# Gated decoder step: natural panels cut as half the contraction by 512 columns, with four token tiles open at once

## The chip, the cores and the metric

The kernel runs on one core of a Trainium2 chip. The metric is the device time of one execution in microseconds (us), here the median of three runs.

## The reference, cut to what matters

One layer for 512 prompt tokens and 8x4 sample tokens, all in float32:

```
h = rmsnorm(x, g_mix);  z = h @ w_in          # 1024 x 7680: [u | va | q | k | v | gate_a | gate_b]
a = gelu(u) * (tril(W_s) @ rmsnorm(gelu(va)) + b)
q, k = rotary(rmsnorm(q, g_q)), rotary(rmsnorm(k, g_k))          # 3 groups x 8 heads x 64
b = softmax over windows of the three groups (dilation 1, 4, 16; samples against cached keys and values)
x += (sigmoid(gate_a) * (a @ w_oa) + sigmoid(gate_b) * (b @ w_ob)) @ w_o
x += relu(rmsnorm(x) @ w_ff1)**2 @ w_ff2
x += sigmoid(rmsnorm(x) @ w_ple_gate) * (p @ w_ple_proj)
```

The new keys and values of the prompt, and the caches of the samples moved on by four positions, are outputs too.

## The kernel before

TensorE (PE) multiplies in split precision: each float32 operand is a rounded part (`_hi`) and a rest (`_lo`), and a product is hi·hi + lo·hi + hi·lo, so three matmuls. ScalarE (ACT) casts a weight half-panel of 128x2x512 or 128x1024 numbers from `w_raw` to `w_hi`, VectorE (DVE) subtracts to get `w_lo`; both buffers hold one panel in two halves of `w_hi`/`w_lo`.

The **natural stage** (us 14 to 346 of the profile) computes q, k and v of three groups and then va, with tokens on the partitions of the result. Its 20 panels are 1024 contraction rows by 256 columns; a pair of panels is one kind of one group (q0, k0, v0, q1, k1, v1, q2, k2, v2, va). A panel has three units: two of two 128-token tiles (48 matmuls of 128x256, lines 1321 to 1323) and one of the sample tokens (16 matmuls with 64 weight columns, lines 1329 and 1330). A unit's output is the PSUM bank `gm[:, u % 3]`: the bank that unit u fills is one that unit u-3 left, and PE waits for `unit_out` at the start of each unit. Scores of the attention (`kT`, `qT`) go to `psS` and to the fourth bank `gm[:, 3]`, transposes to `psT`, value products to `psO`. The profile names `psS` and `psO` alike: `psSO`.

Each engine walks slots written out by hand. In slot s ACT moves unit s out of PSUM (`z<-gm`), squares the heads with a read of the accumulator behind each (`sq<-z`), casts the next half-panels if the slot has them, copies transposes (`PT`, `qT`, `kT`), value products (`O`), and for each score piece exponentiates it (`prob`, twice 128x256 in group 0, four times 128x128 in groups 1 and 2) and writes the mask for the next piece into the bank. DVE multiplies by gain and rotates (`fin`, lines 1820 to 1833), takes row maxima of scores (line 1895), scales by the norm (line 1841), splits `w_lo` (line 1708) and works off one or two **chunks** of the samples' cached keys or values (1024 wide, two instructions each); a table of digits says how many chunks a slot has. `fin` has two buffers; those of k are stored to `kvp` by DMA, and a new rotation waits for the store of two tiles ago (`fin_stored0`, `fin_stored1`). The small PE steps of slot s (transposes `qk` and `pt`, scores, value products) are issued between the matmuls of unit s+1. The stage has 60 slots; the next stage (u, gates, output products) follows, with its own slots and the rest of the chunks, up to us 513. Then comes the feed-forward part, which the change leaves as it is.

```
for job in TJOBS.get(s, []): take_transposes(job)      # ACT, in slot s: behind evacuation, squares and casts
for job in SJOBS.get(s, []): ...                       # then exponentials and masks of the pieces of slot s
```

Of the kernel before, what the change touches and what calls it, by code (L numbers as in the profile page):

```python
# [24 lines left out]
D, SEQ, NB, T = 1024, 512, 8, 4  # L25
# [23 lines left out]
COLS = {"oa": 512, "ob": 512, "pj": 1024}  # L49
UNITS = []  # L50
for _p, (_kind, _g, _i) in enumerate(PANELS):
    _n = 3 if _kind in NATURAL else COLS.get(_kind, 256) // 128
    UNITS += [(_p, _kind, _g, _i, _s) for _s in range(_n)]
U_FF = len(UNITS)
NFF = 4
# [4 lines left out]
for _u, (_p, _kind, _g, _i, _s) in enumerate(UNITS):  # L60
    UNIT[_kind, _i * (COLS.get(_kind, 256) // 128) + _s if _kind not in NATURAL else (_g, _i, _s)] = _u
# [3 lines left out]
def summed_by_act(u):  # L65

    return UNITS[u][1] in ("k", "q")

# [29 lines left out]
def panel_end(p):  # L98

    if p < P_FF:  # L100
        return max(u for u in range(U_FF) if UNITS[u][0] == p) + 1
    return U_FF + 2 * (p - P_FF + 1)

# [76 lines left out]
def late_split(s):  # L180

    _, kind, _, _, sub = UNITS[s]
    return sub == 0 and (kind in NATURAL or kind == "oa")


def stores_heads(u):

    _, kind, g, _, sub = UNITS[u]
    return sub == 2 or (kind == "k" and not (g == 0 and sub == 0))
# [4 lines left out]
PIECE_SLOT = [18 + j for j in range(16)] + [36 + j for j in range(8)] + [54 + j for j in range(8)]  # L194
S_AT = {s: j for j, s in enumerate(PIECE_SLOT)}


def paired(j):

    return j < 30  # L200


def score_bank(j):

    return j % 2 if paired(j) else 0


NEXT_IN_BANK = {j: next((x for x in range(j + 1, len(PIECES)) if score_bank(x) == score_bank(j)), None) for j in range(len(PIECES))}
MASKED_BY_ACT = [x for x in NEXT_IN_BANK.values() if x is not None]

# [3 lines left out]
for _g in range(NG):  # L214
    for _kind in ("keys", "values"):
# [3 lines left out]
CHUNKS_IN_SLOT = ("000000000101202202102102102102213122102102102102112111"  # L219
                  "112103121010030112010100120313200000000000")  # L220
# [20 lines left out]
COPY_AT = [s for s in range(0, 96, 3) if s not in (48, 51, 54, 57)] + [97, 99, 100, 102]  # L241
V_BACK = {35: (1, 0), 39: (1, 1), 53: (2, 0), 57: (2, 1)}


X_STEPS = {10: (2,), 13: (3,), 14: (4,)}
# [4 lines left out]
def _plan_tjobs():  # L250
    n = 0
    order = []
    for s in range(SLOTS):
        if s >= 2 and UNITS[s - 2][1] in ("k", "q") and UNITS[s - 2][4] < 2:
            order.append((s, ("qk", s - 2)))
        if s - 1 in S_AT:
            order.append((s, ("pt", S_AT[s - 1])))
        if s == 53:
            order.append((s, ("ws",)))
        if s == 65:  # L260
            order += [(s, ("mixs",))] + [(s, ("mix", g)) for g in range(4)]
        if s == KEYS_END[2] + 1:
# [7 lines left out]
        if s == 77:  # L270
            order += [(s, ("bt", c)) for c in range(2)]
        if s == 78:
            order += [(s, ("bt", c)) for c in range(2, 4)]
        if 88 <= s < 96:
            order.append((s, ("x", s - 88)))
        if s == 95:
            order.append((s, ("xs",)))
        if 96 <= s < 98:
            order.append((s, ("p", s - 96)))
        if s == 98:  # L280
# [14 lines left out]
def _plan_sjobs():  # L295
    n = 0
    for s in range(SLOTS):
        jobs = []
        if s in S_AT and not (paired(S_AT[s]) and S_AT[s] % 2):
            jobs.append(("piece", S_AT[s]))  # L300
            if paired(S_AT[s]):
                jobs.append(("piece", S_AT[s] + 1))
        for job in jobs:
# [8 lines left out]
def small_steps(s):  # L312

    t, sc = TJOBS.get(s, []), [x for x in SJOBS.get(s, []) if not (paired(x[1]) and x[1] % 2)]
    steps = [("transposes", x) for x in t if x[0] == "qk"] + [("scores", x) for x in sc if x[0] == "piece"]
    steps += [("transposes", x) for x in t if x[0] != "qk"] + [("scores", x) for x in sc if x[0] != "piece"]
# [2223 lines left out]
```

## Time and profile before

| | before |
|---|---|
| median of 3 runs | 1040.69 us (1040.42 to 1045.89) |
| profiled execution, span | 1041.0 us |
| PE busy | 1023.5 us |
| DVE busy | 774.4 us |
| ACT busy | 518.5 us |
| natural stage, 14.14 to 346.00 | 331.86 us, of it PE 328.35, DVE 285.55, ACT 223.25 |
| 346 to 513 | 167.00 us, of it PE 162.82, DVE 150.22 |

The profile comes from one execution, 0.3 us above the median of the runs. Matmuls are pipelined, so a matmul's own duration is longer than the distance to the next; the distance from start to start is what one costs.

### The profile page before, as it was taken

The page shows a single profiled execution, that of the slowest core. Times are in us where ns is not written, and L with a number is a line of the kernel's source. Part 1 is how long each engine was busy: PE and PEld are TensorE (multiplying, and loading weights), DVE is VectorE, ACT ScalarE, POOL GpSimd, SP SyncE. Part 2 cuts the span into 40 slices and gives each one's busy share as a digit, 9 for nine tenths or more (in the row PEclk, how much of TensorE's full clock was granted, in tenths as well). Part 3 has the DMA queues.
Part 4 walks back from the last instruction along what each step waited for, and adds up shares of the span by engine and source line. Part 5 has one row for each costly group of instructions (what it writes and reads, how often), then busy time and mean ns, then how long its engine had stood idle before and what let it go on. Part 6 is the DMA issues. An engine that isn't in the chain of part 4 may idle for free.

```text
span 1041.0 us, 20872 instructions
## 1 busy us (share of the span) xinstructions
PE 1023.5 (98%) x8310; PEld 1008.5 (97%) x8310; DVE 774.4 (74%) x1004; ACT 518.5 (50%) x1253; POOL 245.6 (24%) x381
## 2 busy tenths in 40 slices
PE   9999999999999999999999999999999999999997
PEld 7999999999999999999999989999999999999997
DVE  6679888988899878999674368747856875786553
ACT  6773797658845574352264385414522531453332
POOL 2441233122312003958201211100100100012300
PEclk9999999999999999999999999999999999999999
DMA  6557556776687765776843335655664574573412
GB/s 186 192 178 231 200 177 208 227 242 206 208 256 213 210 218 148 224 218 186 258 142 122 122 122 208 214 183 172 229 209 152 195 247 168 171 252 130 162 54 86
DMA packets 131634, 195.89 MB, mean 188 GB/s; under 512 B 32321, under 2 KB 109473, under 8 KB 129746
## 3 DMA queue, kind: packets, MB, share of 16 engines
q1 hardware_dynamic: 107616, 125.51, 37.9%
q0 software_dynamic: 10560, 63.28, 18.3%
q10 hardware_dynamic: 13362, 5.77, 2.0%
q8 instruction: 66, 1.08, 0.4%
q14 instruction: 30, 0.25, 0.1%
HBM read 185.55 MB, written 62.00 MB: 238 GB/s over the span
## 4 chain that ended last, share of the span: by engine, by line
PE 66%; DVE 13%; ACT 5%; issue 5%; DMA 5%; POOL 3%; SPq 3%; ACTq 0%; DVEq 0%; POOLq 0%
PE gm L1347 26%; PE gm L1603 7%; PE psSO L1603 4%; PE gm L1321 4%; PE gm L1322 3%; PE gm L1323 3%; PE psT L1603 3%; DMA w_raw<-in_w_in 3%; PE psSO L1651 2%; PE psSO L1347 2%; PE psT L1347 2%; PE psT L1651 2%; DVE w_lo L1708 2%; POOL kv L2363 2%; ACT prob L1123 2%
## 5 line engine op out<-in xcount | busy, mean ns | idle before, releaser
L1321 PE MATMUL gm<-w_hi,h_hi 128*128 128x256 f32 x640 | 186.9, 292 | 1.1 <-DVE w_lo L1708 0.9
L1322 PE MATMUL gm<-w_hi,h_lo 128*128 128x256 f32 x640 | 180.8, 282 | 0.0
L1323 PE MATMUL gm<-w_lo,h_hi 128*128 128x256 f32 x640 | 180.1, 281 | 0.0
L1347 PE MATMUL gm<-h_hi,w_hi 128*128 128x272 f32 x624 | 132.7, 294 | 0.4 <-ACT z L852 0.4
L1347 PE MATMUL gm<-h_hi,w_lo 128*128 128x272 f32 x624 | 130.0, 290 | 0.0
L1347 PE MATMUL gm<-h_lo,w_hi 128*128 128x272 f32 x624 | 129.4, 289 | 0.0
L1321 PEld LDWEIGHTS gm<-w_hi,h_hi 128*128 128x128 f32 x640 | 120.8, 189 | 3.1 <-issue 1.7
L1323 PEld LDWEIGHTS gm<-w_lo,h_hi 128*128 128x128 f32 x640 | 121.2, 189 | 0.0
L1322 PEld LDWEIGHTS gm<-w_hi,h_lo 128*128 128x128 f32 x640 | 120.6, 188 | 0.0
L2352 POOL DMA_DIRECT2D out_kvs<-in_cache_kv_w x64 | 35.0, 547 | 345.2 <-PE gm L1347 120.6
L1708 DVE TENSOR_TENSOR w_lo<-w_raw,w_hi 128x1024 fp32r<-128x1024 f32 x76 | 90.5, 1228 | 21.3 <-ACT w_hi L755 20.8
L1347 PEld LDWEIGHTS gm<-h_hi,w_hi 128*128 128x128 f32 x624 | 98.1, 190 | 1.5 <-ACT z L852 0.6
L1347 PEld LDWEIGHTS gm<-h_lo,w_hi 128*128 128x128 f32 x624 | 98.6, 190 | 0.0
L1347 PEld LDWEIGHTS gm<-h_hi,w_lo 128*128 128x128 f32 x624 | 98.2, 190 | 0.0
L755 ACT CAST w_hi<-w_raw 128x1024 fp32r<-128x1024 f32 x76 | 76.8, 1046 | 30.4 <-DMA w_raw<-in_w_in 16.5
L765 ACT CAST w_hi<-w_raw 128x1024 fp32r<-128x1024 f32 x49 | 50.2, 1048 | 82.6 <-PE psSO L1347 28.5
L1347 PE MATMUL gm<-x_hi,w_hi 128*128 128x272 f32 x384 | 80.4, 291 | 0.0
L1347 PE MATMUL gm<-x_hi,w_lo 128*128 128x272 f32 x384 | 79.6, 289 | 0.0
L1347 PE MATMUL gm<-x_lo,w_hi 128*128 128x272 f32 x384 | 79.3, 288 | 0.0
L2363 POOL DMA_DIRECT2D kv<-in_cache_kv_w x128 | 69.4, 708 | 32.8 <-DVE acc L1954 16.8
L1721 DVE TENSOR_TENSOR w_lo<-w_raw,w_hi 128x1024 fp32r<-128x1024 f32 x49 | 59.0, 1221 | 11.9 <-ACT w_hi L765 11.8
L1347 PEld LDWEIGHTS gm<-x_lo,w_hi 128*128 128x128 f32 x384 | 60.4, 189 | 0.0
(378 smaller groups left out, 2662.7 us busy)
## 6 DMA issues: line engine op xcount, KB each, us to landing
out_kvs<-in_cache_kv_w POOLq DMA_DIRECT2D x64, 510.0 KB, 4.7
w_raw<-in_w_in SPq DMA_DIRECT2D x60, 512.0 KB, 6.2
w_raw<-in_w_ff SPq DMA_DIRECT2D x36, 512.0 KB, 5.7
kv<-in_cache_kv_w SPq DMA_DIRECT2D x128, 128.0 KB
kv<-in_cache_kv_w SPq DMA_DIRECT2D x64, 256.0 KB
out_kvs<-in_cache_kv_w POOLq DMA_DIRECT2D x32, 508.0 KB, 5.3
w_more<-in_w_ff SPq DMA_DIRECT2D x26, 512.0 KB, 6.1
kv<-in_cache_kv_w POOLq DMA_DIRECT2D x128, 64.0 KB, 3.3
```

Of the source, the lines that this page charges most:

```text
L755: nc.scalar.copy(w_hi[:, r, hh * 1024:(hh + 1) * 1024], w_raw[:, hh]).then_inc(w_hi_done, 1)
L765: nc.scalar.copy(w_pair(w_hi, PAIRS[p] + n).rearrange("p (k n) -> p k n", k=4), raw(p, hh)).then_inc(w_hi_done, 1)
L1321: nc.tensor.matmul(out, lh, wh, start=k == 0, stop=False)
L1322: nc.tensor.matmul(out, ll, wh, start=False, stop=False)
L1323: last = nc.tensor.matmul(out, lh, wl, start=False, stop=k == KD - 1)
L1347: last = nc.tensor.matmul(pair[:, half, 0:HALF], w, x[:, k0 + k, half * HALF:(half + 1) * HALF], start=first, stop=end)
L1603: last = nc.tensor.matmul(bank[:, 0:HALF], w[wx][:, k], x[xx][:, k], start=start and k == 0 and wx == xx, stop=k == 3 and wx == 1, skip_gr ...
L1651: last = nc.tensor.matmul(banks(u + sub)[:, half, 0:HALF], w, x[:, k, half * HALF:(half + 1) * HALF], start=first, stop=end, skip_group_ch ...
L1708: vec.tensor_tensor(w_lo[:, r, cols], w_raw[:, hh], w_hi[:, r, cols].bitcast(F32), ALU.subtract).then_inc(w_lo_done, 1)
L1721: vec.tensor_tensor(w_pair(w_lo, x).rearrange("p (k n) -> p k n", k=4), raw(p, hh), w_pair(w_hi, x).rearrange("p (k n) -> p k n", k=4).bit ...
L2352: pool.dma_start(dst, src).then_inc(cache_copied, 16)
L2363: pool.dma_start(dst, src).then_inc(late_landed[n % RING], 16)
```

## The change

A natural panel is now 512 contraction rows by 512 columns, so a pair of panels is the two halves of the contraction for all columns of one kind and group. A pair has five **sections** on PE: x=0 is tiles 0 and 1 over the first half, x=1 tiles 2 and 3 over the first half, x=2 the samples over both halves, x=3 tiles 0 and 1 over the second half, x=4 tiles 2 and 3 over the second half. Each tile has its own bank `gm[:, tile]`, open from x=0 or x=1 to x=3 or x=4. Samples go to `psO`, scores to `psS` and `psO`, value products to `psT`. There are 50 natural slots instead of 60. ACT and DVE handle in slot s the unit of two slots ago, in the order samples, t0, t1, t2, t3: tile 2 comes out in slot x=0 of the following pair and tile 3 in its slot x=1. The half-panel for the first half of the next pair is split in slot x=3, the other in slot x=0. Squares of tile 0 and of the samples are one wide Square, summed by DVE; those of tiles 1 to 3 stay as they were. The chunk table has 54 chunks in the natural slots instead of 60, the other six come later. The diff's core:

```diff
+SAMPLES = 4
+TILES = (SAMPLES, 0, 1, 2, 3)
+    elif _i == 1:
+        UNITS += [(_p, _kind, _g, 0, _a) for _a in TILES]
+        SLOT += [(_p - (_x < 2), _kind, _g, 0, _x) for _x in range(5)]
+OUT_OF = {_s: [_s - 2] if 2 <= _s < N0 else [N0 - 2, N0 - 1, N0] if _s == N0 else [_s] if _s > N0 else [] for _s in range(U_FF)}
...
-    return sub == 0 and (kind in NATURAL or kind == "oa")
+    return sub in (0, 3) if s < N0 else sub == 0 and kind == "oa"
...
-PIECE_SLOT = [18 + j for j in range(16)] + [36 + j for j in range(8)] + [54 + j for j in range(8)]
+PAIR_SLOT = [14, 18, 19, 23, 24, 28, 29, 33, 34, 38, 39, 43, 44, 48, 50, 52]
+PT_SLOT = [16, 19, 21, 24, 26, 29, 31, 34, 36, 39, 41, 44, 46, 49, 51, 53]
+PV_SLOT = [17, 20, 22, 25, 27, 30, 32, 35, 37, 40, 42, 45, 48, 50, 52, 54]
...
-CHUNKS_IN_SLOT = ("000000000101202202102102102102213122102102102102112111"
-                  "112103121010030112010100120313200000000000")
+CHUNKS_IN_SLOT = ("00000" "00012" "11213" "22111" "02101" "11213" "22111" "02101" "11213" "21101"
+                  "1211" "1013" "0112" "0102" "1113" "03132000" "00000000")
...
+            def natural_tiles(s):
+                    a = 2 * (x % 3) + n
+                    out, tile = gm[:, a], slice(128 * a, 128 * a + 128)
+                    if half == 0 and first:
+                        pe.wait_ge(unit_out, first - 5 + TILES.index(a) + 1)
...
+                        if n == 0 and x == 0:
+                            panel_split(p, 512, kk)
```

In all, 1,920 matmuls of 128x256 become 960 of 128x512, and 320 sample matmuls of 256 columns become 160 of 512; ACT has 1050 instructions before and 938 after, DVE 1006 and 976.

**ACT, slots 24 and 25** (end of pair k1, start of v1; `PT` is the copy of transposed probabilities, `prob` an exponential, `psSO<-masks` a mask, `z<-gm` the evacuation of tile 2). After the change:

```order
L983 COPY PT<-psT 128x512 [waits t_ready] x2
L1153 ACTIVATE prob<-psSO,O_blk 128x256 [waits t_ready,max_ready]
L1153 ACTIVATE prob<-psSO,O_blk 128x256
L1047 CAST psSO<-masks 128x512 [waits const_in,exp_done]
L1153 ACTIVATE prob<-psSO,O_blk 128x256 [waits t_ready,max_ready]
L1153 ACTIVATE prob<-psSO,O_blk 128x256
L870 COPY z<-gm 128x512 [waits z_used,ssq_ready,unit_ready,exp_done]
L848 ACTIVATE sq,st<-z 128x64 [waits fin_ready,unit_out]
L848 ACTIVATE sq,st<-z 128x64 x7
L782 CAST w_hi<-w_raw 128x1024 [waits unit_ready,w_landed00]
L782 CAST w_hi<-w_raw 128x1024 [waits w_landed01]
L970 COPY kT_59<-psT 128x16x32 [waits t_ready]
```

A place of before with two pieces ahead of an evacuation:

```order
L1123 ACTIVATE prob<-psSO,O_blk 128x256 [waits t_ready,max_ready]
L1123 ACTIVATE prob<-psSO,O_blk 128x256
L1130 CAST psSO<-masks 128x512 [waits const_in,exp_done]
L1123 ACTIVATE prob<-gm,O_blk 128x256 [waits t_ready,max_ready]
L1123 ACTIVATE prob<-gm,O_blk 128x256
L1130 CAST gm<-masks 128x512 [waits const_in,exp_done]
L1029 COPY O_blk<-psSO 128x2x65 [waits pv_ready]
L821 ACTIVATE sq,st<-z 32x64 [waits fin_ready,unit_out]
L821 ACTIVATE sq,st<-z 32x64 x3
L845 COPY z<-gm 128x512 [waits z_used,unit_ready]
```

In both the evacuation stands behind the exponentials. Before, the bank that it frees is for the third unit after; now it is for the section that comes next on PE.

**PE, the end of section x=0 and the start of x=1** in the pair after (v1; `L1482` are the `pt` transposes of slot 24, the row with `unit_out` is the first matmul into tile 2's bank). After:

```order
L1482 MATMUL psT<-ident,prob 128x128 [waits exp_done,t_out]
L1482 MATMUL psT<-ident,prob 128x128 x3
L1347 MATMUL gm<-w_hi,h_hi 128x512
L1348 MATMUL gm<-w_hi,h_lo 128x512
L1349 MATMUL gm<-w_lo,h_hi 128x512
L1347 MATMUL gm<-w_hi,h_hi 128x512
L1348 MATMUL gm<-w_hi,h_lo 128x512
L1349 MATMUL gm<-w_lo,h_hi 128x512
L1347 MATMUL gm<-w_hi,h_hi 128x512 [waits unit_out]
L1348 MATMUL gm<-w_hi,h_lo 128x512
L1349 MATMUL gm<-w_lo,h_hi 128x512
L1475 MATMUL psT<-ident,fin 128x128 [waits fin_ready,t_out]
```

Before, the start of a unit of tiles:

```order
L1321 MATMUL gm<-w_hi,h_hi 128x256
L1322 MATMUL gm<-w_hi,h_lo 128x256
L1323 MATMUL gm<-w_lo,h_hi 128x256
L1321 MATMUL gm<-w_hi,h_hi 128x256 [waits unit_out]
L1322 MATMUL gm<-w_hi,h_lo 128x256
L1323 MATMUL gm<-w_lo,h_hi 128x256
```

What moved: six matmuls lie between the last `pt` transposes, whose copies ACT makes first, and the wait for tile 2's bank.

**DVE, slots 25 and 26** (tile 2 of k1 rotates, `kv` and `acc` are a chunk, `w_lo` the split that the samples section needs from its fifth step on). After:

```order
L1854 TENSOR_TENSOR fin<-z,gk_b 128x512 [waits fin_stored0,t_ready,unit_out]
L1860 TENSOR_TENSOR rot<-fin,cs 128x128 [waits z_used]
L1862 TENSOR_TENSOR rot_136<-fin,cs 128x128
L1864 TENSOR_TENSOR fin<-rot,rot_136 128x8x16 [waits dve_step]
L1983 TENSOR_TENSOR kv<-kv,sc 128x1024 [waits chunk_landed2,dve_step]
L1989 TENSOR_TENSOR acc<-acc,kv 128x1024 [waits values_used,dve_step]
L1744 TENSOR_TENSOR w_lo<-w_raw,w_hi 128x1024 [waits w_hi_done] x2
L1878 TENSOR_TENSOR fin<-fin,st 128x512 [waits rstd_ready]
```

Before, the same kind of place in k1:

```order
L1820 TENSOR_TENSOR fin<-z,gk_b 128x512 [waits fin_stored0,t_ready,unit_out]
L1829 TENSOR_TENSOR rot<-fin,cs 128x128 [waits z_used]
L1831 TENSOR_TENSOR rot_136<-fin,cs 128x128
L1833 TENSOR_TENSOR fin<-rot,rot_136 128x8x16 [waits dve_step]
L1841 TENSOR_TENSOR fs<-fs,st 32x256 [waits rstd_ready,dve_step]
L1948 TENSOR_TENSOR kv<-kv,sc 128x1024 [waits chunk_landed4]
L1954 TENSOR_TENSOR acc<-acc,kv 128x1024 [waits values_used,dve_step]
L1708 TENSOR_TENSOR w_lo<-w_raw,w_hi 128x1024 [waits w_hi_done] x2
```

The rows are alike. What differs is on ACT and PE: tile 0 of k1, whose store the first row waits for, is now transposed in section x=1 of the next pair, and ACT sends its store behind tile 2's evacuation, squares and the two casts.

## Rows read from the trace of the kernel before

**Rows 1.** The page, busy time and share of each engine.
```profile
PE 1023.5 (98%) x8310; PEld 1008.5 (97%) x8310; DVE 774.4 (74%) x1004; ACT 518.5 (50%) x1253; POOL 245.6 (24%) x381
```
**Rows 2.** Busy time by windows, ten pairs of the natural stage; only the sum.
```profile
sum 331.86, PE 328.35 PEld 322.56 DVE 285.55 ACT 223.25 POOL 95.78; mean PE 32.83 PEld 32.26 DVE 28.55 ACT 22.32 POOL 9.58
```
**Rows 3.** Waits of PE: engine, tile, line, releaser: total us, times, longest.
```profile
PE psT L1447 <- ACT prob L1123: 1.5, 2, 0.9
...
PE gm L1321 <- DVE w_lo L1708: 0.9, 1, 0.9
PE psT L1439 <- DVE fin L1841: 0.8, 2, 0.4
```
**Rows 4.** Timeline of PE, two stretches: start us, duration us, instruction.
```profile
160.25 0.28 PE L1322 MATMUL gm<-w_hi,h_lo 128*128 128x256 f32 x1
...
160.96 0.27 PE L1322 MATMUL gm<-w_hi,h_lo 128*128 128x256 f32 x1
...
699.75 0.41 PE L1347 MATMUL gm<-x_hi,w_lo 128*128 128x272 f32 x2
...
700.75 0.41 PE L1347 MATMUL gm<-x_hi,w_hi 128*128 128x272 f32 x2
```
**Rows 5.** Timeline of ACT, a pair of score pieces of group 0.
```profile
161.64 0.84 ACT L1123 ACTIVATE prob<-psSO,O_blk 128x256 f32<-128x256 f32 x2 [0.72 <-DVE O_blk L1895]
...
163.90 0.59 ACT L1130 CAST gm<-masks 128x512 f32<-128x512 bf16 x1
```
**Rows 6.** Timeline of ACT, a pair of score pieces of group 1.
```profile
236.03 1.14 ACT L1123 ACTIVATE prob<-psSO,O 128x128 f32<-128x128 f32 x4 [1.27 <-DVE O L1895]
...
238.89 0.59 ACT L1130 CAST gm<-masks 128x512 f32<-128x512 bf16 x1
```
**Rows 7.** Timeline of ACT, from one tile unit's squares to the next evacuation.
```profile
167.27 0.26 ACT L821 ACTIVATE sq<-z 128x64 f32<-128x64 f32 x1
...
169.20 1.03 ACT L755 CAST w_hi<-w_raw 128x1024 fp32r<-128x1024 f32 x1
...
171.09 0.57 ACT L951 COPY kT<-psT 128x512 f32<-128x512 f32 x1
171.56 0.47 ACT L971 COPY PT<-psT 128x384 f32<-128x384 f32 x1
171.93 0.26 ACT L1029 COPY O_blk<-psSO 128x130 f32<-128x130 f32 x1
172.09 0.58 ACT L845 COPY z<-gm 128x512 f32<-128x512 f32 x1
```
**Rows 8.** Timeline of DVE, two maxima, then a rotation, a chunk and a split.
```profile
160.91 0.69 DVE L1895 TENSOR_REDUCE O_blk<-psSO 128x2 f32<-128x512 f32 x1
...
162.24 1.23 DVE L1948 TENSOR_TENSOR acc<-kv,sc 128x1024 f32<-128x1024 f32 x1
...
167.27 0.69 DVE L1820 TENSOR_TENSOR fin<-z,gk_b 128x512 f32<-128x512 f32 x1 [1.41 <-ACT z L845]
...
168.85 0.41 DVE L1841 TENSOR_TENSOR fs<-fs,st 32x256 f32<-32x256 f32 x1
169.30 1.22 DVE L1948 TENSOR_TENSOR kv<-kv,sc 128x1024 f32<-128x1024 f32 x1
...
171.70 2.35 DVE L1708 TENSOR_TENSOR w_lo<-w_raw,w_hi 128x1024 fp32r<-128x1024 f32 x2
```
**Rows 9.** Line 965, the stores of rotated keys, issue to landing.
```profile
DMA to landing us min/median/max: 4.8/7.0/9.5
```
**Rows 10.** Timeline of PE, transposes and value products between matmuls.
```profile
164.97 0.60 PE L1439 MATMUL psT<-ident,fin 128*128 128x128 f32 x4
...
168.62 1.00 PE L1534 MATMUL psSO<-V,PT 128*128 128x65 f32 x8
```
**Rows 11.** Busy time by windows, 346 to 513, the sum of three.
```profile
sum 167.00, PE 162.82 PEld 160.62 DVE 150.22 ACT 73.58 POOL 81.57; mean PE 54.27 PEld 53.54 DVE 50.07 ACT 24.53 POOL 27.19
```

More of the change, by code:

```diff
@@ L297, in _plan_sjobs @@
     for s in range(SLOTS):
[L298 to L303, printed above, removed]
+        for job in [("piece", j) for j in PAIR_AT.get(s, [])]:
             SJOBS.setdefault(s, []).append(job)
@@ L563, in wait_values @@
         def wait_values(engine, g):
-            for i in range(2):
-                engine.wait_ge(v_stored[g][i], V_STORES[g])
+            engine.wait_ge(v_stored[g], V_STORES[g])
         FIN_STORES = [0, 0, 0]
@@ L1292, in between @@
                     n_steps = len(STEPS[u - 1])
+                    if u < N0 and u % 5 == 1:
+                        groups = 4
                     for n in range(n_steps):
@@ new lines, in natural_tiles @@
+            def natural_tiles(s):
+                p, x = SLOT[s][0], s % 5
+                half, first = x // 3, 5 * (s // 5)
+                for n in range(2):
+                    a = 2 * (x % 3) + n
+                    out, tile = gm[:, a], slice(128 * a, 128 * a + 128)
+                    if half == 0 and first:
+                        pe.wait_ge(unit_out, first - 5 + TILES.index(a) + 1)
+                    if half == 0 and not first:
+                        pe.wait_ge(h_lo_done, 2 * a + 1)
+                    for kk in range(4):
+                        k = 4 * half + kk
+                        if n == 0 and x == 0:
+                            panel_split(p, 512, kk)
+                        wh, wl = w_hi[:, half, kk * 512:kk * 512 + 512], w_lo[:, half, kk * 512:kk * 512 + 512]
+                        nc.tensor.matmul(out, h_hi[:, k, tile], wh, start=k == 0, stop=False, skip_group_check=True)
+                        nc.tensor.matmul(out, h_lo[:, k, tile], wh, start=False, stop=False, skip_group_check=True)
+                        last = nc.tensor.matmul(out, h_hi[:, k, tile], wl, start=False, stop=k == KD - 1, skip_group_check=True)
+                        if 4 * n + kk < 7:
+                            between(s, 4 * n + kk, 8)
+                    if half:
+                        last.then_inc(unit_ready, 1)
@@ new lines, in natural_samples @@
+            def natural_samples(s):
+                p, first = SLOT[s][0], 5 * (s // 5)
+                if first:
+                    pe.wait_ge(unit_out, first - 5 + 1)
+                else:
+                    pe.wait_ge(h_lo_done, KD + 1)
+                if LAST_EXP_BEFORE[s]:
+                    pe.wait_ge(exp_done, LAST_EXP_BEFORE[s])
+                for k in range(KD):
+                    if k >= 4:
+                        panel_split(p, 512, k - 4)
+                    both, cols = hs[k // 4][:, k % 4], slice(k % 4 * 512, k % 4 * 512 + 512)
+                    nc.tensor.matmul(psO[0:2 * NS], both, w_hi[:, k // 4, cols], start=k == 0, stop=False)
+                    last = nc.tensor.matmul(psO[0:2 * NS], both, w_lo[:, k // 4, cols], start=False, stop=k == KD - 1)
+                    if k < KD - 1:
+                        between(s, k, KD)
```

618 lines of the change are left out of this document (302 added, 316 removed).

## The prediction

> **What bounds the kernel now.** I read the page first: PE is busy 98% of the span [rows 1]. PE's waits say why: all of them in the natural stage come to about 3.2 us [rows 3]. So in this stage every other engine is early, and the time is PE's number of matmuls times the distance between them. The windows show that the cover is thin: of 331.9 us PE is busy 328.4 and DVE 285.6, ACT 223.3 [rows 2]. DVE has some 14% of slack, and whatever it does comes just in time. The question is therefore double: how much cheaper the matmuls become, and whether ACT and DVE still answer PE in time, since the banks are now used in another rhythm.
>
> **The matmuls.** In the timeline 128x256 matmuls start 0.71 us apart over six steps, so 118.3 ns each; 128x272 ones 1.00 us over eight, so 125.0 [rows 4]. The 16 columns more cost 6.7 ns, 0.417 ns a column, which is 2.4 GHz. What is left is a fixed 11.6 ns at either width. No fp32r matmul of 512 columns is in the trace. Bounds: with the same fixed part it takes 225.0 ns, with none 213.3. Two narrow ones take 236.6, so each of the 960 + 160 pairs that merge saves 11.6 to 23.3 ns: 13 to 26 us. I take 222 ns, nearer to the 272-column row but not on it, since 272 says little of a width twice as large: 14.6 ns by 1120 is about **−17 us**. The samples are priced as the tiles.
>
> The Trainium skill, *TensorE: Matmul & The Clock Gate*, section "Wait — 56ns, not 53.3ns?", gives N/2.4 GHz plus some 2.5 ns for a warm matmul, 215.7 ns at 512. The trace's 118.3 at 256 disagrees with it, as it would be 109.2. If the page held for the new width only, the saving would be 23 us; if it held for both, 3 us.
>
> **What is late next.** The forecast rests on four places where PE now waits for an answer to something that PE itself has issued a few microseconds before. Such a loop does not get shorter when the engines have slack elsewhere. A group of three wide matmuls is 0.67 us.
>
> *(b) Tile 2's bank, at x=1.* Before, a bank that an evacuation frees is wanted three units on; now tile 2's is wanted one section after x=4. On ACT its evacuation (slot x=0) stands behind what slot x=4 holds: two PT copies, two pieces' exponentials, a mask. The transposes for the second PT copy are issued in section x=0, with two groups of matmuls, 1.33 us, left to the wait. From their end ACT needs 0.1 us to start, 0.5 for the copy (a PT copy's distance to the next, [rows 7], 0.37 to 0.47), 2.26 for exponentials, mask, exponentials of group 0 [rows 5], and 0.59 for the evacuation, with 0.1 to wake PE: 3.5 us, less 1.33 is 2.2. Groups 1 and 2 have 2.86 instead of 2.26 [rows 6]: 2.8. Slots 19, 24, 29 pay 2.2, slots 34, 39, 44 pay 2.8, and slot 14, without a PT copy, some 1.4: **16.4 us**. If the exponentials were through by the time of the copy, the price would be 0 (the copy and evacuation fit in 1.33): that is the other bound.
>
> The Trainium skill, *Perfetto Trace Analysis*, section "Matmuls", asks that independent groups of matmuls rotate through banks so that one's evacuation overlaps the next one's matmuls. The trace agrees: three rotating banks, and PE waits 3.2 us in the stage. By that rule four banks that all come back at once speak against the change.
>
> *(c) Tile 3's bank, halfway through x=1.* After tile 2's evacuation ACT does tile 2's squares (1.93), two casts (1.89), a transposed copy (0.47), two O copies (0.16 each) and then tile 3's evacuation (0.58) [rows 7]: 5.2 us and 0.3 of handing over. PE has in the meantime twelve matmuls (2.66), four transposes (0.44) and eight value products (0.83; [rows 10], first duration and the distances): 3.9. Stall 1.6 in q1, k1, q2, k2. In q0 and k0 there are no value products on either side: 1.9. v and va have no such squares. Sum **10 us**; the least is 1.0 each time (O copy, evacuation, handing over behind the last value product), 6 us.
>
> *(a) First-half weights, at x=0.* The scores of slot x=3 are issued in section x=4 with three groups left (2.0 us; four, 2.67, in slots 18 and 33). DVE must take two maxima (1.33), in q and k scale the samples' heads (0.6, an estimate between the 0.41 of 32x256 and twice that), in slot 18 half a chunk and in 33 a whole one (2.4), and then split the first half (1.2) [rows 8]; 0.3 for handing over. Slots 18, 23, 28, 33, 38, 43 come to 2.0, 1.5, 0.9, 3.2, 1.5, 0.9: **10 us**. Nothing if DVE had its split ahead of the maxima; by the order of the code it has not.
>
> *(d) Second-half weights, in the samples of v1 and v2.* Tile 0 of k1 and k2 is transposed at the start of x=1, and ACT sends its store behind tile 2's squares, casts and copy, 4.3 us on [rows 7]. The store lands 7.0 us later (4.8 to 9.5) [rows 9], at 11.4 after the start of x=1. DVE's rotation of tile 2 waits for it, and behind it stand the rotation (1.6), a chunk (2.4) and the split (1.2) that the samples' fifth step needs: ready at 16.6. PE is there at about 10.5 (3.9, the stall of 1.6, 2.7 of tile 3, 1.8 of samples, 0.5 of transposes). Stall 6.1 each, **12 us**, between 8 and 17 by the extremes of the landing.
>
> **Other terms.** The 3.2 us of old waits belong to places that no longer exist: −3. ACT loses 48 wide-tile head squares and the half of the samples'; they were under PE's time, at no price. DVE's twelve added sums of 0.6 us are hidden by its slack. Weight loads have the same bytes in fewer, longer rows; the half-panels are asked for a section earlier than needed, so at nothing; without that cover a load's tail would add to (a). From 346 to 513, DVE is busy 150 of 167 [rows 11], and six chunks (2 x 1.2 us each, 15 us) move there, with wide gelus of va and a pair of maxima, 18 in all. It has 17 idle, and after 49 us of stalls on PE it enters the stage with nothing left over, where before it entered late. I price this at nothing, with up to 12 in the range.
>
> **Sum.** 16.4 + 10 + 10 + 12 = 48 of new stalls, −17, −3: +28. The profiled execution has 1041.0, 0.3 above the median, so the forecast is 1069.
>
> **The rivals.**
> *Faster: the answers come in time.* For it: before, the same engines answered the same kinds of question with 3.2 us of waits, and ACT is half idle. Then the matmuls' saving stands: 1041 − 17 = 1024 (1015 with the full 26; 1031 if 7 us of waits remain). Against it: the order rows, where nothing but six matmuls lies between the last transposes and the wait. It decides at (b): if the evacuation of tile 2 ends less than 1.3 us after those transposes, the loop is closed.
> *Only some loops bind.* If, say, (b) and (c) bind at their lower half and (a) and (d) hide behind each other, 16 to 25 us of stalls against 20 saved: 1037 to 1046, and up to 1055 with 34.
> *DVE limits what follows too.* If the chunks moved find no room, 5 to 20 us come on top: 1080 to 1089.
> *The narrow matmul's fixed part is not the wide one's.* This is in the bounds above, −26 to −13. By the skill's formula for both widths the saving would be 3 us and the time 1083; the 11.6 ns in the rows speak against it.
>
> **How the numbers follow.** This kernel's measurement tells 0.5%, 5 us, from no change. Chances: forecast (1055 to 1080) 0.55; some loops (1036 to 1055) 0.19; faster (under 1036) 0.19, of it some 0.12 under 1030; DVE or dear matmuls (over 1080) 0.07. Slower is all of the first and the last and the upper half of the second; same is 0.09. The likeliest is 1069; the range leaves out the two tails: 1030 to 1086.
>
> **What would show it.** The pitch of 128x512 matmuls, 213 to 225 ns. PE's waits in the natural stage, some 48 us in place of 3: on ACT's `z` at L1347 with two lengths, 2.2 and 1.6, in each pair; on DVE's `w_lo` at L1347 around 1 to 3 us six times; on `w_lo` at L1368 some 6 us twice, with DVE's `fin` waiting for `out_kvp`. PE busy falls in the stage from 328 to some 310. The prediction is wrong if ACT's exponentials run ahead of the PT copies' end in time, if the store lands far faster than 7 us, or if a stall at one place pays for the next, so that the four don't add.

## The result and the profile after

The changed kernel takes 1110.83 us, median of four runs (1108.96 to 1113.51), beside 1043.08 (1040.42 to 1045.89) for the kernel before on the same chip: 1.0647 times as long [1.0608, 1.0685]. The direction was forecast, the size was not: 1110.83 lies 25 us above the range. The profiled execution has a span of 1108.1 us, 67.1 more than before.

The page's line of busy times, to be read against [rows 1]:

```profile
PE 1040.5 (94%) x7189; PEld 955.0 (86%) x7190; DVE 777.5 (70%) x974; ACT 491.5 (44%) x1061; POOL 239.5 (22%) x366
```

PE has 1,121 fewer instructions recorded and is busy 17 us longer; DVE has 3 us more work than it had and ACT 27 less, and the share of both falls. So hardly anything was added to the other engines: everyone waits longer for the others. The window of the natural stage after, from its first matmul to the start of the first u unit (us, busy time of PE, PEld, DVE, ACT, POOL with the number of instructions, then the granted clock, DMA share, GB/s):

```profile
14.13:393.90 379.77, 339.31 (x1737) 264.08 (x1738) 282.56 (x378) 195.38 (x595) 85.35 (x88) 0.96 0.57 186
```

[rows 2] end at 346.00, and the kernel before has 4.5 us of the stage left there. To the start of its first u unit the stage takes 336.3 us before, with PE busy 332.8, DVE 290.0 and ACT 226.1, at a granted clock of 1.00. So PE's busy time rose in the stage, to 339, where I had forecast some 310.

The first u unit starts at 393.92 instead of 350.45: 43.4 us are lost by then. Another 22.4 are lost by the first matmul of the feed-forward part (708.9 and 643.1), and 1.3 behind it. PE's waits from 14 to 394 (engine, tile, line, releaser: total us, times, longest), to be read against [rows 3]:

```profile
PE gm L1347 <- DVE w_lo L1744: 11.0, 7, 5.0
PE gm L1347 <- ACT z L870: 9.8, 5, 2.6
PE psT L1562 <- DMA V<-out_kvp: 6.9, 1, 6.9
PE gm L1347 <- ACT V L885: 5.3, 3, 2.6
PE gm L1385 <- ACT z L870: 3.9, 1, 3.9
...
PE psT L1570 <- ACT qT L970: 0.8, 1, 0.8
```

With the small ones these are 40.1 us where there were 3.3: 36.8 of the 43.4. And from 394 to 600, where before had some 4:

```profile
PE psT L1489 <- DVE sc L1961: 8.4, 1, 8.4
PE gm L1385 <- ACT z L870: 6.2, 2, 3.9
PE gm L1385 <- DVE w_lo L1744: 4.2, 3, 1.9
```

(The 3.9 us at 393.92 stand in both windows.)

**The loop at tile 2.** ACT, then PE, at the start of v1 (start us, us, instruction, idle before it and who ended it):

```profile
186.19 0.59 ACT L983 COPY PT<-psT 128x512 f32<-128x512 f32 x1 [1.24 <-PE psT L1482]
186.68 0.84 ACT L1153 ACTIVATE prob<-psSO,O_blk 128x256 f32<-128x256 f32 x2
...
188.94 0.59 ACT L870 COPY z<-gm 128x512 f32<-128x512 f32 x1
...
189.58 0.51 PE L1347 MATMUL gm<-w_hi,h_hi 128*128 128x512 f32 x1 [2.03 <-ACT z L870]
```

ACT had itself waited 1.24 us for PE's transposes. Then come a copy, exponentials, a mask, exponentials and only then the copy that frees the bank, and PE starts 0.05 us behind that copy's end. From 186.19 to 189.58 nothing on ACT is idle: a half-idle engine is the bound for 3.4 us.

**The pitch.** Two starts on PE, nine matmuls of 512 columns apart, all of them uninterrupted:

```profile
46.06 0.40 PE L1347 MATMUL gm<-w_hi,h_hi 128*128 128x512 f32 x1
...
48.14 0.39 PE L1347 MATMUL gm<-w_hi,h_hi 128*128 128x512 f32 x1
```

2.08 us by 9 are 231 ns; the median over the stage is 232. Two narrow matmuls cost 236.6 [rows 4], so a pair that merges saves about 5 ns, not 14.6.

**After some waits PE runs at half its clock.** PE behind the longest wait for weights, and the window row of that stretch:

```profile
136.88 0.77 PE L1347 MATMUL gm<-w_hi,h_hi 128*128 128x512 f32 x1 [5.04 <-DVE w_lo L1744]
137.45 0.63 PE L1348 MATMUL gm<-w_hi,h_lo 128*128 128x512 f32 x1
137.88 0.63 PE L1349 MATMUL gm<-w_lo,h_hi 128*128 128x512 f32 x1
...
136.50:140.00 3.50, 3.12 (x8) 2.11 (x10) 3.40 (x8) 1.80 (x16) 1.52 (x2) 0.50 0.54 146
```

The matmuls start 430 ns apart, and the granted clock is 0.50, 1.2 GHz; at that clock the 512 columns take 427 ns, by the 0.417 ns that a column takes at full clock [rows 4]. It does not follow every wait: behind those of 2.64 us at 269.86 and 311.22 the granted clock stays 1.00, behind those of 2.03 to 2.34 us at 149.38, 189.58 and 229.11 it falls.

Over the stage the granted clock averages 0.96, where it was 1.00 before. In the half-clock stretches of the stage the wide matmuls cost some 7 us above their normal distances. The small steps there (transposes, scores, value products) cost 4.5 us above what the same runs of steps take elsewhere: eight value products take 1.70 us to the next matmul at 382.77 and 0.81 at 194.72. That is why PE's busy time rose.

So the 43.4 us are 36.8 of waits and some 11 of half clock, less the 5 that the wide matmuls save.

**The border of the stage.** PE's two stalls there, ACT and DVE around them (sorted by what follows from what):

```profile
382.77 1.94 PE L1562 MATMUL psT<-V,PT 128*128 128x65 f32 x8 [6.86 <-DMA V<-out_kvp]
384.75 0.38 ACT L1041 COPY O<-psT 128x260 f32<-128x260 f32 x1 [6.24 <-PE psT L1562]
...
392.94 0.69 DVE L1917 SCALAR_TENSOR_TENSOR va<-sq,z 128x512 f32<-128x512 f32 x1 [12.06 <-ACT sq L928]
393.29 0.58 ACT L870 COPY z<-gm 128x512 f32<-128x512 f32 x1
393.92 0.52 PE L1385 MATMUL gm<-h_hi,w_hi 128*128 128x272 f32 x2 [3.90 <-ACT z L870]
...
401.91 0.59 ACT L870 COPY z<-gm 128x512 f32<-128x512 f32 x1
404.97 0.76 PE L1385 MATMUL gm<-h_hi,w_hi 128*128 128x272 f32 x2 [2.32 <-ACT z L870]
```

Here one late transfer stops all three engines in turn: values that come back from memory hold PE 6.86 us, ACT's copy of the product waits behind PE 6.24, and the gelu of va, further back on ACT, leaves DVE idle for 12.06. The copies that empty va's tiles come behind that, at 393.29 and 401.91, so the banks that the first u units want are not there.

### The profile page after: what moved, and what is told of

The parts are those of the page before. It is cut to its first block, busy times and chain, and to the rows that moved or that the text cites. A ratio compares the mean times of both kernels' runs of the same rounds, so it can differ in the third digit from the quotient of the medians.

```text
span 1108.1 us, 18328 instructions
## 1 busy us (share of the span) xinstructions
PE 1040.5 (94%) x7189; PEld 955.0 (86%) x7190; DVE 777.5 (70%) x974; ACT 491.5 (44%) x1061; POOL 239.5 (22%) x366
## 4 chain that ended last, share of the span: by engine, by line
PE 69%; DVE 13%; ACT 5%; issue 5%; POOL 3%; DMA 3%; SPq 2%; ACTq 0%; DVEq 0%; POOLq 0%
PE gm L1385 22%; PE gm L1639 6%; PE gm L1347 5%; PE gm L1348 5%; PE gm L1349 5%; PE psSO L1639 3%; PE psT L1639 2%; DVE w_lo L1744 2%; POOL kv L2410 2%; PE psSO L1687 2%; PE psSO L1385 2%; PE psT L1385 2%; PE psT L1687 2%; DVE kv L1942 2%; PE psSO L1544 1%
## 5 line engine op out<-in xcount | busy, mean ns | idle before, releaser
L1347 PE MATMUL gm<-w_hi,h_hi 128*128 128x512 f32 x320 | 137.4, 429 | 26.9 <-DVE w_lo L1744 11.0
L1385 PE MATMUL gm<-h_hi,w_hi 128*128 128x272 f32 x624 | 135.3, 299 | 9.1 <-ACT z L870 6.2
L1348 PE MATMUL gm<-w_hi,h_lo 128*128 128x512 f32 x320 | 128.5, 402 | 0.0
L1349 PE MATMUL gm<-w_lo,h_hi 128*128 128x512 f32 x320 | 128.4, 401 | 0.0
L1347 PEld LDWEIGHTS gm<-w_hi,h_hi 128*128 128x128 f32 x320 | 61.6, 192 | 47.8 <-ACT z L870 19.5
L1349 PEld LDWEIGHTS gm<-w_lo,h_hi 128*128 128x128 f32 x320 | 61.8, 193 | 14.7
L1348 PEld LDWEIGHTS gm<-w_hi,h_lo 128*128 128x128 f32 x320 | 61.9, 193 | 10.1
L1757 DVE TENSOR_TENSOR w_lo<-w_raw,w_hi 128x1024 fp32r<-128x1024 f32 x49 | 59.0, 1220 | 11.6 <-ACT w_hi L792 11.4
L1385 PEld LDWEIGHTS gm<-x_hi,w_hi 128*128 128x128 f32 x384 | 60.2, 188 | 2.0 <-issue 2.0
```

The source lines that it names most:

```text
L1347: nc.tensor.matmul(out, h_hi[:, k, tile], wh, start=k == 0, stop=False, skip_group_check=True)
L1348: nc.tensor.matmul(out, h_lo[:, k, tile], wh, start=False, stop=False, skip_group_check=True)
L1349: last = nc.tensor.matmul(out, h_hi[:, k, tile], wl, start=False, stop=k == KD - 1, skip_group_check=True)
L1385: last = nc.tensor.matmul(pair[:, half, 0:HALF], w, x[:, k0 + k, half * HALF:(half + 1) * HALF], start=first, stop=end)
L1757: vec.tensor_tensor(w_pair(w_lo, x).rearrange("p (k n) -> p k n", k=4), raw(p, hh), w_pair(w_hi, x).rearrange("p (k n) -> p k n", k=4).bit ...
```

## The experiments

All ratios are to the kernel before, on the same chip; the changed kernel stands at 1.0647. The experiments' kernels start from the changed kernel.

### One loop opened at a time

**Tile 2 (and 3) copied out early.** A copy of `z` or `V` without the squares goes to slot x=4, ahead of the `PT` copies and exponentials; `t23_early` does it for tiles 2 and 3.

```diff
+                if s % 5 == 4 and s < N0:
+                    for u in (s - 1, s):
+                        if moved_early(u):
+                            copy_out(u)
                 for job in TJOBS.get(s, []):
                     take_transposes(job)
```

> The changed kernel with one move on ACT: tile 2 is copied out of its bank in slot x=4, ahead of that slot's transposed copies and exponentials, and not in slot x=0 behind them; everything else stays. Theory of the loops: the seven waits of 1 to 3 us at the start of x=1 (16 us together) go, but tile 3's evacuation still stands behind exponentials, squares and casts, so PE meets the same ACT chain half a section later; tile 3's waits grow from 0.3 to about 2 us each, and the time falls by only 4 to 7 us, to 1104 to 1107. Rival, a single late evacuation is the whole matter: the 16 us are gained, 1095 or less. Rival, ACT has too much work in all: no change within 3 us.

> As before it, with tile 3 copied out in slot x=4 too, ahead of the exponentials. Theory of the loops: PE's waits for ACT at x=1 (16 us) and half a section later (3 us with the transposed copies) go to under 3 us, and some 4 us of half-clock matmuls behind them; time 1111 to about 1088, between 1083 and 1095. Rival, ACT is short of time in all: the waits move to scores, probabilities or casts, and the gain is under 8 us.

Measured: t2_early 1115.79 us, 1.0690 [1.0660, 1.0721]; t23_early 1113.56, 1.0671 [1.0641, 1.0701]. No gain, though the waits for `z` and `V` at L1371 are gone in t23_early (t2_early keeps 1.5 us of them). PE's waits of t23_early:

```profile
PE gm L1371 <- DVE w_lo L1768: 13.8, 7, 6.0
PE psT L1586 <- DMA V<-out_kvp: 10.8, 1, 10.8
...
PE psT L1594 <- ACT qT L990: 5.9, 2, 3.1
PE psT L1586 <- ACT kT L990: 3.1, 1, 3.1
PE psT L1594 <- ACT kT L990: 2.5, 1, 2.5
```

The 15.1 us of `z` and `V` turned up as 2.8 more for `w_lo`, 3.9 more for `V`'s return and some 10 more for the value products, which share `psT` with the transposed heads and wait until ACT has copied those. The granted clock over the natural stage is 0.94, beside 0.96, and the wide matmuls at half clock cost 12 us in place of 7. ACT's chain at this place is only in another order; that it is no shorter is argued from the order, not measured.

**The split ahead of the maxima.** DVE, in slots x=3:

```diff
+                ahead = s < N0 and s % 5 == 3
+                if ahead:
+                    split_lo(p + 1, (p + 1) % 2)
                 for job in SJOBS.get(s, []):
                     take_scores(job)
```

> The changed kernel with one move on DVE: in slots x=3 the split of the next pair's first half stands ahead of the row maxima, not behind them, the sample scaling and the chunk. Theory of the loops: PE's six waits for w_lo at x=0 (11 us) go; maxima come 2.3 us later, but the exponentials of x=3 are not what tile 2 waits for, so nothing is given back; with the clock behind the 5.4 us wait the time falls by 10 to 15 us, to 1096 to 1101. Rival, a shift: later maxima make exponentials, mask and tile 2's evacuation later, the waits for ACT grow by as much, and the time stays within 4 us of 1111.

Measured: 1102.27 us, 1.0577 [1.0544, 1.0610], −8.6. The wait for `w_lo` falls from 11.0 to 1.7, and another takes most of its place, since the maxima now stand behind the split, and with them the exponentials and the mask that PE's next scores need:

```profile
PE psSO L1544 <- ACT psSO L1047: 8.9, 6, 3.0
```

**ACT's order rewritten.** `reorder` is t23_early with the cast of slot x=0 moved up to slot x=4 and the squares of tiles 2 and 3 behind the transposed copies; `reorder_split` adds the split ahead.

```diff
+                    if s + 1 < N0:
+                        q = SLOT[s + 1][0]
+                        split_hi(q + 1, (q + 1) % 2, ...)
                 for job in TJOBS.get(s, []):
                     take_transposes(job)
+                for o in later:
+                    evacuate(o)
```

> The early copies of tiles 2 and 3 showed the wait going to the value products, which share the transposes' two buffers and so stand behind ACT's copy of transposed heads, and that behind squares and casts. Here ACT's order is changed throughout: in slot x=4 tiles 2 and 3 are copied out and the second half-panel is cast ahead of the PT copies and exponentials, and the squares of tiles 2 and 3 come behind the copies of heads and value products. Theory of one chain on ACT (scores, exponentials, squares, casts, copy of heads, value products): with 4 us of it taken out the waits at x=1 (15 us of z and V, or 12 us of value products) go to under 4 us and the half-clock matmuls behind them with them; 1111 to 1088 to 1095. Rival, the waits move once more, to scores, masks or w_lo: 1103 or more.

> The same order on ACT, and on DVE the split of the first half ahead of the maxima in slots x=3. If the two chains are separate, their gains add: w_lo's 11 us go too, and the time is 1076 to 1084. If later maxima push exponentials and masks back into the section that follows (PE waited 8.9 us for masks when only the split was moved), no more than 5 us come on top of the reordering alone.

Measured: 1104.37, 1.0584 [1.0547, 1.0621], and 1100.95, 1.0558 [1.0521, 1.0595]. −6.5 and −8.6 apart, −9.9 together: they don't add. In reorder `w_lo` stands at 17.5 us; in reorder_split it falls to 4.4 and the masks have most of it:

```profile
PE psSO L1577 <- ACT psSO L1069: 10.4, 6, 3.6
```

**The values' return.** Before, a group's values came back from memory in two halves, wanted at different times; after, they come as a whole, asked for at 369.2 and landed at 382.6. `pv_late` moves the last three transposed copies and the last four steps of value products one slot on:

```diff
-PT_SLOT = [..., 46, 49, 51, 53]
-PV_SLOT = [..., 45, 48, 50, 52, 54]
+PT_SLOT = [..., 46, 50, 52, 54]
+PV_SLOT = [..., 45, 49, 51, 53, 55]
```

> The changed kernel with the last four pairs' transposes and value products one slot later (PT slots 50, 52, 54 for 49, 51, 53, PV slots 49, 51, 53, 55 for 48, 50, 52, 54). PE waits 6.9 us in va for the values of group 2, which go out to memory and come back. Theory, a new wait of its own: those 7 us go, 1111 to 1104, or 1101 with the half clock behind. Rival: the evacuation of va's tiles, for which PE waits 4.3 and 2.6 us right behind it, takes the place, and the time stays at 1108 to 1111.

Measured: 1099.79 us, 1.0546 [1.0520, 1.0571]: −11.0. The wait of 6.9 is gone, and more than its own length with it. In the profiled executions the first u unit starts 4.7 us earlier and the whole is 9.5 us shorter, so about half of the gain lies behind the border. DVE's waits for the gelu of va fall from 18.0 us (longest 12.1) to 7.8 (longest 4.9), but the first u units wait for `z` as before (7.3 us, 6.2 in the changed kernel): the late values are not what keeps those banks, and what made the rest of the gain was not shown.

**PE's small steps closer together.** In sections x=4 and x=0 the transposes, scores and value products are spread over the first four and six groups of matmuls, in place of all eight, so that more matmuls stand between a question and the wait for its answer:

```diff
-                    if u < N0 and u % 5 == 1:
+                    if u < N0 and u % 5 in (1, 4):
                         groups = 4
+                    elif 0 < u < N0 and u % 5 == 0:
+                        groups = 6
```

> The changed kernel with the small steps at other places between PE's own matmuls, nothing else: in section x=4 the transposes and scores come at groups 1 and 2 of 8 (2 and 5 now, or 4 for scores alone), in x=0 scores and transposes at 1, 3, 4 (2, 4, 6 now). No engine's work changes. Theory of the loops: every answer has 1.3 to 2 us more to arrive; of the w_lo waits at x=0 (11 us) 9 go, of the ACT waits at x=1 (15 us) 9 go, and 5 us of half-clock matmuls behind them; 1111 to 1086 to 1093. Rival, ACT and DVE have too much work per pair wherever it is put: the waits move to scores, masks and transposes, and less than 6 us are gained.

Measured: 1093.55 us, 1.0476 [1.0431, 1.0522]: −17.3, the largest of the single edits; 12.7 between the two profiled executions. PE's waits:

```profile
PE psT L1564 <- DMA V<-out_kvp: 10.5, 1, 10.5
...
PE gm L1349 <- DVE w_lo L1746: 6.8, 4, 4.9
PE psT L1572 <- ACT qT L970: 6.1, 2, 5.3
PE gm L1349 <- ACT z L870: 4.3, 5, 1.2
```

`z` and `V` fall from 15.1 to 6.2 (4.3 and 1.9), `w_lo` from 11.0 to 6.8. Both come down at once here, since the question is put earlier and not one answer moved ahead of another. Two waits take part of it back: the return of `V` 3.6, and the copy of the transposed heads `qT` 5.3 (6.1 in place of 0.8), behind which value products stand. PE's waits in the natural stage fall by some 7 us in all, and the wide matmuls at half clock by another 3.

### The matmul and the chunks

**Two narrow matmuls in place of a wide one.** The changed kernel with its order, panels and banks, every tile matmul cut at 256 columns:

```diff
+                        for c in (slice(0, 256), slice(256, 512)):
+                            nc.tensor.matmul(out[:, c], h_hi[:, k, tile], wh[:, c], ...)
```

> The changed kernel with each 128x512 matmul of a tile issued as two of 128x256 into the halves of its bank (1,920 again), all else as it was. It prices the merging alone. By the trace of the changed kernel (232 ns for one wide against 118.4 for a narrow one) a pair costs 237, 5 ns more: 960 x 5 is 5 us on PE, of which some lies in the waits: 1111 to 1116. By the term of the prediction (14.6 ns a pair): 14 us more, 1121 to 1125.

Measured: 1115.00 us, 1.0693 [1.0667, 1.0718]: +4.2 for 960 pairs, 4.4 ns each, which is what the pitches give. The two intervals touch, and waits and half clock differ between the two executions by as much, so the pitches are the firmer evidence. Its own pitch, twelve steps:

```profile
45.93 0.28 PE L1349 MATMUL gm<-w_hi,h_hi 128*128 128x256 f32 x1
...
47.36 0.28 PE L1349 MATMUL gm<-w_hi,h_hi 128*128 128x256 f32 x1
```

1.43 us by 12 are 119 ns, as [rows 4]. By the pitches, all of the width's gain is 4 to 5 us.

**The six chunks back in the natural slots.**

```diff
-... "11213" "21101" "1211" "1013" "0112" ...
+... "11214" "22213" "0111" "1011" "0011" ...
```

Here one chunk of group-1 values stands ahead of the softmax of its weights, so the samples' attention differs; the amount of work is the same.

> The changed kernel with six chunks taken back from slots 50 to 58 into slots 44 to 49, 60 in the natural slots as before the change. Theory: DVE idles there beside a waiting PE and is behind by the time of slot 69, where PE waits 8.4 us for it; the 8.4 us go and some 4 us of w_lo waits, 1111 to 1098 to 1102. Rival: the chunks delay splits and rotations in v2 and va by the same 14 us, and the time stays within 4 us of 1111.

Measured: 1106.63 us, 1.0619 [1.0588, 1.0650], −4.2, which is not clear of the intervals. The wait for `sc` falls from 8.4 to 5.9 and the first u units' wait for `w_lo` from 4.2 to 1.9, while the natural stage grows by 4.6. The place of the six chunks explains at most a small part of the 22 us.

**The chunks out of slots x=2 and x=3.** `spread` leaves the number per stage as it is, but none stands between the last maxima and the split:

```diff
-"00000" "00012" "11213" "22111" "02101" "11213" "22111" "02101" "11213" "21101"
+"00000" "00012" "22004" "22002" "22001" "22004" "22003" "12001" "22004" "21101"
```

> The changed kernel with the same chunks in the same pairs, but none in slots x=2 and x=3, where DVE joins and rotates the samples and tile 0 and the maxima and the split stand behind; they are in x=4, x=0 and x=1 instead. Theory, DVE's queue in front of maxima and split is what PE waits for at x=0: 2.4 to 4.8 us less stand there, the 11 us of w_lo waits fall to 3 to 5, and the time to 1098 to 1104. Rival, DVE has too much in any place: waits appear at the samples' second half (w_lo at L1368) or at transposes of heads, and the time stays within 4 us of 1111.

Measured: 1107.41 us, 1.0606 [1.0573, 1.0638], −3.4, not clear of the intervals either. `w_lo` comes down from 11.0 (longest 5.0) to 6.3 (longest 2.5), and 3.0 of that return behind masks:

```profile
PE gm L1347 <- DVE w_lo L1744: 6.3, 8, 2.5
...
PE psSO L1544 <- ACT psSO L1047: 3.4, 4, 1.6
```

### Edits in company

Each is a sum of the edits above: steps = early_steps, split = split_first, pv = pv_late, chunks = the table of spread with the six chunks back, spread_all = all but narrow and the six chunks.

> Early steps with the split ahead of the maxima and the late value products. If the waits are loops, what each of the three gains alone (early steps some 20, split 9, value products 11) adds but for the w_lo part that the first two share: 1076 to 1083. If they move from one place to the next, 1090 or more.

> All of it, with ACT's other order as well (copies of tiles 2 and 3 and the cast early, squares late). Loops: what remains of the waits at x=1 goes, 1068 to 1077, still slower than the kernel before, as some 25 us stand outside the natural loops (DVE's lag behind its chunks in the next stage 8, the first two units' banks 6, more half-clock matmuls). Rival as above: 1088 or more.

> Everything: spread chunks, early steps, late value products, split ahead of the maxima, and ACT's other order. In the same kernel without the spread PE waits 15.6 us for masks, eight times, behind exponentials that wait for maxima that wait for DVE's samples, a chunk, tile 0 and the split. Theory of DVE's queue: with the chunk gone from there the masks' waits fall by 2 us each, to 3 to 5 us, 1095 to 1080 to 1085. Rival, exponentials and masks of two neighbouring sections follow each other too closely in two banks whatever DVE does: no less than 10 us of mask waits remain and the time is 1090 or more.

> Spread chunks with early small steps and late value products, in the given order on ACT and DVE. Theory of DVE's queue: early steps alone still waited 6.8 us for w_lo, 6 of ACT's heads and 10 of the values of group 2; 1094 falls by 4 of w_lo and 8 to 11 of the values, to 1079 to 1083. Rival: 1088 or more.

> Spread chunks, early steps and late value products, and six chunks from slots 50 to 58 taken back into slots 46 to 49 (60 in the natural slots, as before the change). Theory: what is left behind the natural stage, 22 us against the kernel before, is DVE's lag behind its chunks; the waits for DVE's sums (7.7) and splits (4.0) there shrink, 1077 to 1068 to 1072. Rival: 15 us more of DVE work in va is 15 us more of waiting in va, 1077 or more.

> The same kernel with spread chunks, early steps and late value products, and each 128x512 matmul of a tile as two of 128x256. It prices the merging where less waiting hides it: 960 x 5 ns is 5 us, 1080 to 1083. By the prediction's term it would be 14 us, 1089 to 1093.

| kernel | us | ratio |
|---|---|---|
| steps_split_pv | 1094.33 | 1.0478 [1.0449, 1.0508] |
| steps_reorder_split_pv | 1094.91 | 1.0495 [1.0465, 1.0524] |
| spread_all | 1092.32 | 1.0454 [1.0433, 1.0475] |
| spread_steps_pv | 1077.07 | 1.0316 [1.0292, 1.0339] |
| spread_steps_pv_chunks | 1079.59 | 1.0372 [1.0328, 1.0416] |
| spread_steps_pv_narrow | 1081.09 | 1.0372 [1.0337, 1.0407] |

Steps, pv and spread save 17.3, 11.0 and 3.4 alone, 31.7 in sum, and 33.8 together: they add. The window of the natural stage in spread_steps_pv:

```profile
14.13:362.80 348.67, 326.00 (x1722) 253.57 (x1723) 281.65 (x378) 194.58 (x593) 87.77 (x88) 1.00 0.61 197
```

The stage is 31.1 us shorter than in the changed kernel. PE's waits fall by some 17, and the half clock is gone from it: the granted clock is 1.00, and no wide matmul starts at the half-clock distance. With the split ahead and ACT's new order the same three edits stand at 1092.32, 15 us worse: these two take from one answer what they give to another. Where it goes, in spread_all:

```profile
PE psSO L1579 <- ACT psSO L1069: 18.9, 11, 3.0
```

The waits left in the best one, spread_steps_pv, over 14 to 600:

```profile
PE psT L1491 <- DVE sc L1963: 7.7, 1, 7.7
PE gm L1387 <- ACT z L870: 6.8, 2, 4.7
...
PE gm L1387 <- DVE w_lo L1746: 4.0, 2, 2.2
```

Its first u unit starts at 362.8, 12.3 us behind before's; some 20 us are lost after that. The rows of `sc`, and of `z` and `w_lo` at L1387, 18.5 us, belong to that stage (4.75 of `z` just ahead of its first unit), where before had some 4. With the six chunks back as well, `sc` falls to 5.2 and `z` at the first units rises to 9.1. The narrow form is 4.0 us slower here by the medians and some 6 by the ratios. No version is as fast as the kernel before. Of the six expectations, the rival's price came true in steps_split_pv, steps_reorder_split_pv, spread_all and spread_steps_pv_chunks; spread_steps_pv came out 2 us below the range of its theory, and the narrow form inside its own.

## Why the prediction was right or wrong

**Right: the direction and its cause.** PE waits in loops for answers to questions that it put a few microseconds earlier, while ACT is busy 44% of the span and DVE 70%. The rival that the answers come in time decided at 1.3 us behind the transposes; by the rows at 186.19 the chain takes 3.4.

**(b) Tile 2's bank: right.** 16.4 forecast. The eight waits for `z` and `V` at L1347 make 15.1; seven of them are tile 2's, 14.8 in all: 0.7, 2.3, 2.0, 2.0, 2.6, 2.6 and 2.6, with 1.4, then 2.2, then 2.8 forecast.

**(a) First-half weights: right in sum, by luck in part.** 10 forecast, 11.0 measured; slot 18 alone has 5.0, where I had put 2.0, and the other five stay below their forecasts. DVE in slot 18:

```profile
132.16 1.28 DVE L1930 TENSOR_REDUCE O_blk<-psSO 128x2 f32<-128x512 f32 x2
...
135.52 2.35 DVE L1744 TENSOR_TENSOR w_lo<-w_raw,w_hi 128x1024 fp32r<-128x1024 f32 x2
```

PE's scores for it run from 127.71 to about 128.8, but DVE takes the maxima 3.4 us later, behind a chunk and a rotation. I had counted DVE as free when the scores end.

**(c) Tile 3's bank: the size failed.** I wrote "PE has in the meantime twelve matmuls (2.66), four transposes (0.44) and eight value products (0.83)", 3.9 us, and so a stall of 1.6. What the eight rows leave for tile 3 is 0.3 us, and value products behind `kT` and `qT` take 1.6. PE and ACT in v1:

```profile
192.82 1.30 PE L1570 MATMUL psT<-V,PT 128*128 128x65 f32 x8
...
194.72 1.00 PE L1570 MATMUL psT<-V,PT 128*128 128x65 f32 x8
...
195.75 0.27 ACT L1041 COPY O_blk<-psT 128x130 f32<-128x130 f32 x1 [1.33 <-PE psT L1570]
```

There are two sets of eight value products between the two tiles, one for each of the two O copies, and I had counted one: 0.8 us more for PE. In v1 PE needs 7.0 us from tile 2's start (189.58) to tile 3's (196.56), about 2 of them for half clock, and ACT waits for PE here, 1.33 us. At 269.86, where the granted clock stays 1.00, PE still needs some 5.5 us beside its wait of 0.8 for `qT`. So it was PE's own time, put at 3.9, that hid ACT's chain of 5.5.

**(d) Second-half weights in the samples: the size failed.** I wrote that ACT sends the store "behind tile 2's squares, casts and copy", and that it lands 7.0 us later. ACT's queue, its next datapath work, then DVE and PE, in v1, and the landing of these stores:

```profile
191.78 0.35 ACTq L977 DMA_DIRECT2D out_kvp<-fin  x1
...
193.37 0.57 ACT L970 COPY kT<-psT 128x512 f32<-128x512 f32 x1
...
194.30 0.69 DVE L1854 TENSOR_TENSOR fin<-z,gk_b 128x512 f32<-128x512 f32 x1 [7.15 <-DMA out_kvp<-fin]
...
198.28 2.35 DVE L1744 TENSOR_TENSOR w_lo<-w_raw,w_hi 128x1024 fp32r<-128x1024 f32 x2
...
199.44 0.40 PE L1368 MATMUL psSO<-w_hi,hs 128*64 128x512 f32 x1
...
DMA to landing us min/median/max: 2.4/4.6/5.7
```

The wait on DVE is there, 7.15 us, but the store left 2.2 us after tile 2's start and not 4.3, ahead of a copy that precedes it in the code, and had landed by 194.30, 2.5 us later. The split begins at 198.28; its first half is through about when the samples begin, and PE does not wait. 12 forecast, 0 measured.

**The matmuls: the saving was put too high.** I took 222 ns from bounds of 213 to 225; it is 232, outside them. "With the same fixed part" was the wrong upper bound: what does not belong to the columns is 11.6 ns at 256 columns and 18.7 at 512. −17 became −5. The Trainium skill, *TensorE: Matmul & The Clock Gate*, section "Wait — 56ns, not 53.3ns?", would give 215.7 at 512; the trace disagrees at this width as at 256.

**What no term had.** Three things:
- The values' return, 6.9 us in the profile and 11.0 in time. The diff shows that a group's values come back whole, and I didn't ask when they are wanted.
- The half clock after a stall: some 11 us in the natural stage, which had none before, and some 8 more behind it. I had added stalls as if PE resumed at full speed.
- The stage from 346 to 513: "I price this at nothing, with up to 12 in the range". It cost 22.4 us. The reason given, that DVE "enters the stage with nothing left over", did not hold: before the border DVE stood idle 12.06 us for a gelu of va behind ACT's copies, and va's tiles left their banks after the next stage had begun. The nearest of the rivals was "DVE limits what follows too", 5 to 20 us at a chance of 0.07: in the window from 505 to 560 DVE is busy 54.1 of 55.0 us, and PE waits 8.4 us there for `sc`. But taking back the six chunks, which that rival named as the reason, gained no more than 4 us.

In all, (c) and (d) were 20 us too large. Matmuls (12), the values' return (6.9), the first u unit's bank (3.9) and half clock (11) in the stage, and what lies behind it (24), were 58 too small. The difference is the 39 us by which the sum fell short.

**What the experiments settle.** The doubt that was named, that "a stall at one place pays for the next", is the main thing learnt: freeing banks earlier gains nothing (t2_early, t23_early), taking one answer ahead of another gains a part (split_first, reorder), and more distance between question and wait gains most (early_steps) and still gains in company. Part of these differences is half clock, which no pair of runs holds fixed. The width was worth 4 to 5 us by the pitches, and two pairs of runs agree with it within their noise.

**What stays open.** Of the 22.4 us behind the start of the first u unit PE's waits make about 12 over before (16.3 against some 4), half clock some 8 (granted clock 0.96 there, 0.99 before), and small steps that moved over the border some 2. Why DVE's `sc` comes late was not settled, nor were va's late banks and the late softmax of the samples tried by themselves. Bringing the chunks forward moved the time by −4.2 in one company and +2.5 in the other, neither clear of the noise.

## What to carry to other kernels

When buffers rotate by one and one, the reuse distance is whole units; when four of them open and close together, every reuse waits on what was issued last, and a half-idle engine becomes the bound for the length of its chain. Look in the changed order for each wait whose answer depends on PE's own last few instructions, and lengthen that distance; moving one answer ahead of another on the same engine moved most of the wait elsewhere here. And price a wider matmul from a row of that width, and a stall with the slow matmuls that can follow it.

## What the runs showed of the hardware

- A matmul of 512 columns in these rounded operands starts 231 to 232 ns after the one before, one of 256 columns 118 to 119: the part beyond the columns is not constant.
- After a wait of 5.04 us the granted clock was 0.50 and matmuls started 430 ns apart; after one of 2.03 us they started 0.34 to 0.43 us apart, and the last at 0.43 stands 2.8 us behind its end. After two waits of 2.64 us the granted clock stayed 1.00.
- A store issued from ACT's queue left at 191.78, ahead of a copy at 193.37 that precedes it in the code, while ACT's casts were still running.
